# Activations placed 96 bytes (modulo 256) from the weights in SBUF, in place of 192

## The chip, the cores and the metric

The kernel is one program on one core of a Trainium2 chip. The metric is the device time of one execution in microseconds. The two timed runs of the kernel before took 2176.17 and 2174.1 us, median 2175.14 us.

## The reference, cut to what matters

A batch of one, 256 tokens, model width 2048, everything in float32, passes through three layers in a row:

```python
def reference(x, ...):
    x = first_block(x, ...)         # mLSTM + gated conv mixer, w_out, conv FFN (D_FF 5504), norm
    x = second_block(x, ...)        # GLA mixer, then MLA attention, each x + rms_norm(y)
    return x

# the bulk of it is products of 256 tokens with float32 weights, such as
proj = hn @ w_in + b_in                       # 2048 -> q, k, v, o, gates, conv parts, merge gates
h = h + merged @ w_out
u = causal_dwconv(hn @ w_up, ffn_conv_w, ffn_conv_b)
h = h + (silu(gate) * val) @ w_down
proj = h @ l0_gla_w_in;  y = (o * silu(gate)) @ l0_gla_w_out
proj = h @ l1_mla_w_in;  y = (o * silu(gate)) @ l1_mla_w_out
```

The weights are about 390 MB of float32 and each is used once.

## The kernel before, in words

**Layout.** Features lie on the 128 partitions and the 256 tokens (`T`) along the free dimension. An activation of 2048 features is `[P, 16, 256]` float32; feature tile k is 1024 contiguous bytes in each partition.

**Weights.** The host lays all weights out as one stream of 370 chunks of 1 MB (`stream_in`), in the order of use. SyncE loads chunk after chunk into `raw` (L533). A chunk is two units of `[128, 1024]` float32, a unit is eight weight tiles of 128x128. ScalarE rounds each unit to `w_hi` in the format fp32r (L955), and VectorE writes the rest, `raw - w_hi`, to `w_lo` (L1385). `raw`, `w_hi` and `w_lo` are rings of four units. The activations are split in the same manner into a high and a low part (`n_hi`/`n_lo`, `mg_hi`/`mg_lo`, `f_hi`/`f_lo`, `og_hi`/`og_lo`, `c_hi`/`c_lo`, `mo_hi`/`mo_lo`, `hm_*`, `yc_*`).

**The products.** The function `tile` (L574 to L576) makes one weight tile's product of three matmuls into the same PSUM bank: high weights by high activations, high weights by low activations, low weights by high activations. Each matmul loads its own 128x128 stationary operand (a weight tile; 512 bytes in each partition) and streams 256 columns of activations (1024 bytes in each partition). This is called a triple below. `feature_tile` strings 16 such triples together, and its helpers the others. `token_tiles` (L619 to L621) does the values of the mixers the other way round: the activation tile is stationary and 256 or 512 columns of weights stream. The small attention products (`att`) are plain float32 matmuls.

**The order.** It is written out by hand on each engine, in the order of the table `PHASES`: gates, mix (four heads), merge, wout, wup, wdown, rank, gla (four heads), glaout, latent, krope, mla (four groups), mlaout. TensorE waits for the split of a weight unit (`lo_ready`), for activations, and for its PSUM bank to be emptied (`acc_taken`).

**Addresses.** The tensors made with `sb` (L111 to L132) follow one another in each partition: `x`, `raw`, `w_hi`, `w_lo`, then the filler `apart`, which nothing reads or writes, then `n_hi`, `n_lo`, the parameters and the small constants. Each of the large ones is a multiple of 256 bytes long. `x` starts at byte 16512, which is 128 modulo 256, and so do `raw`, `w_hi` and `w_lo`. `apart` is 192 bytes, so `n_hi` and `n_lo` start at 64 modulo 256. All other tensors are placed by `Arena` from `arena_start` (L135) on, which is rounded up to 64 modulo 256 (byte 130368); their sizes are nearly all multiples of 256 bytes, so every activation that streams also starts at 64 modulo 256. `LINE` is 256. `par` is 2296 bytes and is followed at 64 modulo 256 again by `normed`, `square` and the rest; `ones`, `ident` and `ones_r` lie 64 bytes further (after `g_both`).

Of the kernel before, what the change touches and what calls it, by code (L numbers as in the profile page):

```python
# [18 lines left out]
P = 128  # L19
# [18 lines left out]
LINE = 256  # L38
# [29 lines left out]
def program(nc, x_in, stream_in, params_in, v_bias_in, gk2_in, positions_in, out):  # L68
# [26 lines left out]
    with ctx:  # L95
        def sb(name, shape, dt=fp32):
            return ctx.enter_context(nc.sbuf_tensor(name, shape, dt))
# [14 lines left out]
        raw = sb("raw", [P, RING, UNIT])  # L112
        w_hi = sb("w_hi", [P, RING, UNIT], fp32r)
        w_lo = sb("w_lo", [P, RING, UNIT], fp32r)
        apart = sb("apart", [P, LINE // 4 * 3 // 4])
        n_hi = sb("n_hi", [P, KT, T], fp32r)
        n_lo = sb("n_lo", [P, KT, T], fp32r)
        par = sb("par", [P, N_PARAMS])
# [13 lines left out]
        eps_eps_col = sb("eps_eps_col", [P, 1])  # L132


        arena_start = -(-(nc.sbuf_base - LINE // 4) // LINE) * LINE + LINE // 4  # L135
        arena_end = nc.sbuf_usable_end

        class Arena:
# [2163 lines left out]
```

How the kernel before makes its waits and increments, by code:

```python
        def taken(eng, b, name, i, j):  # L465
            eng.wait_ge(acc_taken[b], FREE + count(1 + b, name, i, j + 1))
# [32 lines left out]
            def wait(self):  # L501
                self.eng.wait_ge(self.steps, self.n if self.i is None else self.i * self.per + self.n)
# [19 lines left out]
        @block.sync  # L522
# [7 lines left out]
            def load(n, slot, source):  # L530
                sp.wait_ge(lo_ready, 2 * n - 2)
                sp.dma_start(raw[:, 2 * slot:2 * slot + 2, :],
                             stream_in[source].rearrange("p (u n) -> p u n", u=2)).then_inc(raw_ready[slot], 16)
# [5 lines left out]
                    load(2 * i + c, c, 2 * i + c)  # L540
            with sp.Fori(0, A_HEADS // 4) as i:
                for c, source in enumerate((2, 0, 1, 3, 4, 5, 6, 7)):
                    load(8 * i + (mla_at + c), c % 2, 8 * i + (mla_at + source))
            with sp.Fori(mla_end // 2, N_CHUNKS // 2) as i:
                for c in range(2):
                    load(2 * i + c, c, 2 * i + c)
            for g in range(KT // 4):
                sp.wait_ge(x_added, FREE + KT // 4 + g + 1)
                sp.wait_ge(x_added_pool, FREE + KT // 4 + g + 1)
                sp.dma_start(out[:, 4 * g:4 * g + 4, :], x[:, 4 * g:4 * g + 4, :]).then_inc(stored, 16)
            sp.wait_ge(stored, 16 * (KT // 4))
# [4 lines left out]
            def unit(name, i, j):  # L558
                u, s, _ = unit_of(name, i, j)
                pe.wait_ge(lo_ready, u + 1)
                return s
# [307 lines left out]
            def scores(i, n):  # L870
                pe.wait_ge(qrope_ready, FREE + 8 * i + 4 * (n // 2 + 1))
```

## Time and profile before

| | |
|---|---|
| median of the timed runs | 2175.14 us |
| the profiled execution | 2177.88 us, its span 2175.8 us |
| mean granted TensorE clock | 0.987 |
| busy, share of the span: TensorE / weight loads / VectorE / ScalarE / GpSimd | 97% / 95% / 60% / 53% / 13% |
| DMA | 393.83 MB, mean 181 GB/s, queue busy 50.4% |
| triples by their activations (matmuls at L574) | `n` 3488, `f` 688, `og`, `mo` and `mg` 256 each, `c` 160, `hm` and `yc` 128 each: 5360 in all |
| matmuls of `token_tiles` | 384 of 256 columns, 480 of 512 columns |

Two things help in reading it. A matmul's record lasts from its start to the end of its passage through the array, while the next one starts long before: what a matmul costs in a dense stream is the step from one start to the next, and that is the length of a stretch divided by the matmuls that started in it. The lines of the trace count in a stretch also the two or three matmuls that were under way when it began. And the granted clock has two levels, 1.00 (2.4 GHz) and 0.50 (1.2 GHz).

### The profile page before, as it was taken

To read this page: it belongs to the slowest core of one execution; us is meant where nothing else is said; L and a number is where in the kernel's file an instruction comes from. 1 tells how busy PE (TensorE), PEld (TensorE's weight loads), DVE (VectorE), ACT (ScalarE), POOL (GpSimd) and SP (SyncE) were. 2 spreads that over 40 slices of the span, in tenths; PEclk is the share of its full clock that TensorE was granted. 3 is DMA by queue.
4 is the path that set the end of the run, shared out by engine and by line. 5 is a ranking of instruction groups with operands and counts; after the bars stand their busy time and mean duration, and the time that the engine had idled before them with its cause. 6 is when DMAs were issued, how large, how long until landed. Compare 5 with 4: busy or idle time off the path is not lost.

```text
span 2175.8 us, 46737 instructions
## 1 busy us (share of the span) xinstructions
PE 2110.0 (97%) x17596; PEld 2071.1 (95%) x17596; DVE 1313.0 (60%) x1662; ACT 1159.3 (53%) x1558; POOL 280.0 (13%) x325
## 2 busy tenths in 40 slices
PE   5999999999999999999999999999999979999996
PEld 5999999999999999999999999999998969999996
DVE  5656655444457777777775555575665565766644
ACT  5444545555445656565655444645555445566643
POOL 2000000000110111111111101111001123111112
PEclk8999999999999999999999999999999989999998
DMA  4455455555555555555555655455444533444443
GB/s 153 170 179 190 172 175 197 185 200 193 185 188 206 193 193 193 193 193 193 193 193 195 224 218 209 173 180 194 174 158 171 192 135 136 175 154 156 171 174 116
DMA packets 54927, 393.83 MB, mean 181 GB/s; under 512 B 6097, under 2 KB 6225, under 8 KB 7522
## 3 DMA queue, kind: packets, MB, share of 16 engines
q1 hardware_dynamic: 54432, 392.19, 50.4%
q10 hardware_dynamic: 450, 1.02, 0.1%
q8 instruction: 31, 0.51, 0.1%
q14 instruction: 14, 0.11, 0.0%
HBM read 391.09 MB, written 2.10 MB: 181 GB/s over the span
## 4 chain that ended last, share of the span: by engine, by line
PE 83%; issue 11%; DVE 2%; POOL 2%; ACT 1%; DMA 0%; DVEq 0%; POOLq 0%; ACTq 0%; SPq 0%
PE acc L574 24%; PE acc L575 24%; PE acc L576 24%; PE tok L619 2%; PE tok L621 2%; PE tok L620 2%; POOL sumsq_g L1983 1%; PE att L647 1%; POOL n_lo L1992 0%; PE att L878 0%; PE att L879 0%; POOL x L2005 0%; DVE w_lo L1385 0%; DVE rstd L1393 0%; PE att L821 0%
## 5 line engine op out<-in xcount | busy, mean ns | idle before, releaser
L1385 DVE TENSOR_TENSOR w_lo<-raw,w_hi 128x1024 fp32r<-128x1024 f32 x740 | 904.1, 1235 | 710.9 <-ACT w_hi L955 708.5
L955 ACT ACTIVATE w_hi<-raw 128x1024 fp32r<-128x1024 f32 x740 | 768.3, 1056 | 552.1 <-PE acc L576 295.1
L574 PE MATMUL acc<-n_hi,w_hi 128*128 128x256 f32 x3488 | 974.2, 279 | 23.9 <-POOL n_lo L1992 20.3
L575 PE MATMUL acc<-n_lo,w_hi 128*128 128x256 f32 x3488 | 968.7, 278 | 0.0
L576 PE MATMUL acc<-n_hi,w_lo 128*128 128x256 f32 x3488 | 968.6, 278 | 0.0
L574 PEld LDWEIGHTS acc<-n_hi,w_hi 128*128 128x128 f32 x3488 | 658.9, 189 | 27.3 <-issue 20.5
L575 PEld LDWEIGHTS acc<-n_lo,w_hi 128*128 128x128 f32 x3488 | 659.7, 189 | 0.5
L576 PEld LDWEIGHTS acc<-n_hi,w_lo 128*128 128x128 f32 x3488 | 658.9, 189 | 0.0
L574 PE MATMUL acc<-f_hi,w_hi 128*128 128x256 f32 x688 | 189.9, 276 | 0.0
L575 PE MATMUL acc<-f_lo,w_hi 128*128 128x256 f32 x688 | 189.9, 276 | 0.0
L576 PE MATMUL acc<-f_hi,w_lo 128*128 128x256 f32 x688 | 189.9, 276 | 0.0
L576 PEld LDWEIGHTS acc<-f_hi,w_lo 128*128 128x128 f32 x688 | 129.2, 188 | 0.0
L574 PEld LDWEIGHTS acc<-f_hi,w_hi 128*128 128x128 f32 x688 | 129.2, 188 | 0.0
L575 PEld LDWEIGHTS acc<-f_lo,w_hi 128*128 128x128 f32 x688 | 129.2, 188 | 0.0
L2059 POOL TENSOR_TENSOR f_lo<-f_act,f_hi 128x256 f32 x43 | 57.8, 1344 | 413.7 <-ACT f_hi L1142 413.7
L1981 POOL TENSOR_TENSOR sumsq<-sumsq,square 128x256 f32<-128x256 f32 x64 | 47.3, 739 | 436.5 <-ACT square L964 228.7
L619 PE MATMUL tok<-w_hi,n_hi 128*128 128x256 f32 (+1 forms) x256 | 86.8, 339 | 0.0
L621 PE MATMUL tok<-w_hi,n_lo 128*128 128x256 f32 (+1 forms) x256 | 86.7, 339 | 0.0
L620 PE MATMUL tok<-w_lo,n_hi 128*128 128x256 f32 (+1 forms) x256 | 86.6, 338 | 0.0
L574 PE MATMUL acc<-og_hi,w_hi 128*128 128x256 f32 x256 | 72.0, 281 | 2.4 <-DVE og_lo L1696 2.4
L574 PE MATMUL acc<-mo_hi,w_hi 128*128 128x256 f32 x256 | 72.0, 281 | 0.0
L575 PE MATMUL acc<-mo_lo,w_hi 128*128 128x256 f32 x256 | 71.9, 281 | 0.0
(324 smaller groups left out, 2959.7 us busy)
## 6 DMA issues: line engine op xcount, KB each, us to landing
raw<-stream_in SPq DMA_DIRECT2D x370, 1024.0 KB, 4.8
x<-x_in SPq DMA_DIRECT2D x4, 512.0 KB, 7.6
out<-x SPq DMA_DIRECT2D x4, 512.0 KB, 2.7
v_bias<-v_bias_in ACTq DMA_DIRECT2D x1, 512.0 KB, 8.9
par<-params_in ACTq DMA_DIRECT2D x1, 287.0 KB, 5.5
pos_i<-positions_in ACTq DMA_DIRECT2D x1, 128.0 KB, 6.8
gk<-gk_in ACTq DMA_DIRECT2D x1, 68.0 KB
```

What stands on the lines that cost most here:

```text
L574: nc.tensor.matmul(out, w_hi[:, s, wc], hi[:, k, :], start=first, stop=False)
L575: nc.tensor.matmul(out, w_hi[:, s, wc], lo[:, k, :], start=False, stop=False)
L576: return nc.tensor.matmul(out, w_lo[:, s, wc], hi[:, k, :], start=False, stop=last)
L619: nc.tensor.matmul(o, hi[:, k0 + k, tt], w_hi[:, s, wc], start=k == 0, stop=False)
L620: nc.tensor.matmul(o, hi[:, k0 + k, tt], w_lo[:, s, wc], start=False, stop=False)
L621: last = nc.tensor.matmul(o, lo[:, k0 + k, tt], w_hi[:, s, wc], start=False, stop=k == n_k - 1)
L647: last = nc.tensor.matmul(att[3][:, 0:T], ones[:, :], squares_all[:, k, :], start=k == 0, stop=k == KT - 1)
L955: nc.scalar.activation(w_hi[:, s, :], raw[:, s, :], ACT.Copy).then_inc(hi_ready, 1)
L1385: nc.vector.tensor_tensor(w_lo[:, s, :], raw[:, s, :], w_hi[:, s, :].bitcast(fp32), ALU.subtract).then_inc(lo_ready, 1)
L1981: ins = gp.tensor_tensor(sumsq[:, :], sumsq[:, :], square[:, m, :], ALU.add)
L1983: ins = gp.tensor_tensor(sumsq_g[:, :], sumsq_g[:, :], square_g[:, m, :], ALU.add)
L2059: gp.tensor_tensor(f_lo[:, i, :], f_act[:, :], f_hi[:, i, :].bitcast(fp32), ALU.subtract)\
```

## The change

The filler becomes 96 bytes, and the arena's start is rounded up to 224 modulo 256 in place of 64:

```diff
         w_lo = sb("w_lo", [P, RING, UNIT], fp32r)
-        apart = sb("apart", [P, LINE // 4 * 3 // 4])
+        apart = sb("apart", [P, LINE // 4 * 3 // 8])
         n_hi = sb("n_hi", [P, KT, T], fp32r)
...
-        arena_start = -(-(nc.sbuf_base - LINE // 4) // LINE) * LINE + LINE // 4
+        arena_start = -(-(nc.sbuf_base - LINE * 7 // 8) // LINE) * LINE + LINE * 7 // 8
```

`x`, `raw`, `w_hi` and `w_lo` stay where they are (128 modulo 256). `n_hi`, `n_lo` and all that follows them, and the whole arena, move down by 96 bytes: the arena starts at byte 130272 in place of 130368, and the streamed activations at 224 modulo 256 in place of 64. Relative to the weights that is 96 in place of 192. Where the weights stream and the activation is stationary (`token_tiles`), the distance from stationary to streamed operand goes from 64 to 160. Distances between two tensors of the arena, and between `n_hi` and `ones`, stay as they were. No instruction is added, removed or moved on any engine, and each queue issues the same transfers in the same order.

## Rows read from the trace of the kernel before

**Rows 1.** The page: the span; busy time, share and instructions of the engines.
```profile
span 2175.8 us, 46737 instructions
PE 2110.0 (97%) x17596; PEld 2071.1 (95%) x17596; DVE 1313.0 (60%) x1662; ACT 1159.3 (53%) x1558; POOL 280.0 (13%) x325
```

**Rows 2.** The page: the chain that ended last, by engine.
```profile
PE 83%; issue 11%; DVE 2%; POOL 2%; ACT 1%; DMA 0%; DVEq 0%; POOLq 0%; ACTq 0%; SPq 0%
```

**Rows 3.** Groups of instructions: xcount, busy us, mean ns of one, idle before.
```profile
L574 PE MATMUL acc<-n_hi,w_hi 128*128 128x256 f32 x3488 | 974.2, 279 | 23.9 <-POOL n_lo L1992 20.3 <-issue 3.6
L575 PE MATMUL acc<-f_lo,w_hi 128*128 128x256 f32 x688 | 189.9, 276 | 0.0
L575 PE MATMUL acc<-og_lo,w_hi 128*128 128x256 f32 x256 | 71.9, 281 | 0.0
```

**Rows 4.** By stretch: us, then PE, PEld, DVE, ACT, POOL busy (x); clock, DMA.
```profile
44.00:308.00 264.00, 263.43 (x2199) 258.76 (x2199) 156.98 (x183) 130.91 (x164) 15.50 (x13) 0.99 0.49 174
310.00:1382.00 1072.00, 1072.00 (x9461) 1072.00 (x9460) 658.70 (x814) 586.34 (x748) 120.00 (x130) 1.00 0.55 197
1403.00:1681.00 278.00, 277.81 (x2100) 259.43 (x2098) 174.14 (x240) 147.94 (x182) 29.53 (x20) 1.00 0.50 178
1684.00:1768.00 84.00, 84.00 (x716) 84.00 (x715) 41.50 (x45) 39.66 (x60) 11.11 (x15) 1.00 0.53 188
1803.00:2065.00 262.00, 258.14 (x2038) 250.41 (x2039) 166.29 (x246) 156.55 (x259) 50.79 (x80) 1.00 0.45 162
2067.00:2156.00 89.00, 89.00 (x758) 89.00 (x758) 34.29 (x29) 38.92 (x60) 12.50 (x18) 1.00 0.43 153
```

**Rows 5.** Timeline of TensorE from 799.7 us (start us, length us), wup stage.
```profile
799.74 0.28 PE L575 MATMUL acc<-n_lo,w_hi 128*128 128x256 f32 x1
799.85 0.28 PE L576 MATMUL acc<-n_hi,w_lo 128*128 128x256 f32 x1
...
800.53 0.28 PE L576 MATMUL acc<-n_hi,w_lo 128*128 128x256 f32 x1
```

**Rows 6.** Timeline of the weight loads in the same stretch.
```profile
799.85 0.19 PEld L574 LDWEIGHTS acc<-n_hi,w_hi 128*128 128x128 f32 x1
...
800.53 0.19 PEld L574 LDWEIGHTS acc<-n_hi,w_hi 128*128 128x128 f32 x1
```

**Rows 7.** Timeline of TensorE from 40.1 us, granted clock 0.50.
```profile
40.11 0.41 PE L576 MATMUL acc<-n_hi,w_lo 128*128 128x256 f32 x1
...
41.39 0.41 PE L576 MATMUL acc<-n_hi,w_lo 128*128 128x256 f32 x1
```

**Rows 8.** Groups at L575 in the stretches 44:308, 1403:1681 and 1803:2065.
```profile
L575 PE MATMUL acc<-n_lo,w_hi 128*128 128x256 f32 x573 | 159.3, 278 | 0.0
...
L575 PE MATMUL acc<-n_lo,w_hi 128*128 128x256 f32 x488 | 134.9, 276 | 0.0
...
L575 PE MATMUL acc<-n_lo,w_hi 128*128 128x256 f32 x408 | 113.6, 278 | 0.0
L575 PE MATMUL acc<-c_lo,w_hi 128*128 128x256 f32 x160 | 44.8, 280 | 0.0
```

**Rows 9.** Timeline of TensorE from 307.8 us: the last small product before the long stretch.
```profile
307.30 0.60 PE L695 MATMUL att<-h_sum,ones 128*128 128x256 f32 x2
...
308.08 0.28 PE L574 MATMUL acc<-n_hi,w_hi 128*128 128x256 f32 x1
308.21 0.28 PE L575 MATMUL acc<-n_lo,w_hi 128*128 128x256 f32 x1
308.32 0.28 PE L576 MATMUL acc<-n_hi,w_lo 128*128 128x256 f32 x1
```

**Rows 10.** Timeline of TensorE from 1419.8 us: `token_tiles` of 512 columns.
```profile
1419.76 0.39 PE L619 MATMUL tok<-w_hi,n_hi 128*128 128x512 f32 x1
...
1420.91 0.39 PE L621 MATMUL tok<-w_hi,n_lo 128*128 128x512 f32 x1
```

**Rows 11.** VectorE's groups that read from one and two elements off a tile's start.
```profile
L1619 DVE SCALAR_TENSOR_TENSOR f_val<-f_pre,par,f_val 128x255 f32<-128x255 f32 x43 | 20.6, 478 | 0.0
L1623 DVE SCALAR_TENSOR_TENSOR f_val<-f_pre,par,f_val 128x254 f32<-128x254 f32 x43 | 20.8, 483 | 6.1 <-DVE f_val L1619 0.2
```

## The prediction

> **What bounds the kernel now.** I read the page first. TensorE is busy 97% of the span with 17596 matmuls [rows 1], and the chain that ended last runs 83% through it, with 11% of issue, which here is time between matmuls that waited for nothing [rows 2]. TensorE's idle time before the largest group is 23.9 us of the whole [rows 3]. So the time is the number of matmuls times the step from one start to the next, and the change can act only through that step, or through a wait that does not exist now.
>
> Next come the stretches [rows 4]. From 310 to 1382 us (merge, wout, wup, wdown) TensorE never stops: 1072 us for 9461 matmuls less the three already under way, a **fast step of 113.3 ns**. From 1684 to 1768 us (glaout) it never stops either, and there it is 84 us for 713: a **slow step of 117.8 ns**. From 2067 to 2156 us (mlaout), 89 us for 755, it is 117.9 ns. The granted clock is 1.00 in all three. The timeline shows the fast step at close hand, seven steps in 0.79 us [rows 5], with a weight load starting beside every matmul [rows 6]. The record of one matmul lasts 276 ns at the fast step and 281 ns at the slow one, as the groups of `f` and `og` show [rows 3], and that tells the two apart where a stretch is mixed.
>
> What is the least such a step could be? At a granted clock of 0.50 the same matmuls start every 213.3 ns (1.28 us for six [rows 7]), which is exactly 256 columns at 1.2 GHz. At 2.4 GHz the columns alone would be **106.7 ns**. So 6.7 ns of the fast step and 11.1 ns of the slow one are something that doesn't show at half the clock. `f`, `mg` and `og` all start at the same address modulo 256 and are used by the same code, yet two steps exist, and each is kept for hundreds or thousands of matmuls. The step is thus not set by addresses alone: the stream falls into one of two rhythms, and changes it at an interruption. The long fast stretch began right after a small product, with one odd step of 0.13 us [rows 9], and the rhythm then held until 1382 us.
>
> **How many matmuls run at which step.** 5360 triples are 16,080 matmuls. Fast are the 9,458 of the long stretch and the gla stretch's 488 x 3 = 1,464, whose records last 276 ns. In the mix stretch the mean is 159.3 / 573 = 278.0 ns, so (281 - 278.0) / 5 = 60% of 1,719 are fast, 1,031; in the mla stretch 113.6 / 408 = 278.4 gives 52% of 1,224, 636, and `c` at 280 gives 20% of 480, 96 [rows 8]. That is 12,685 fast. About 110 ran at half the clock at the beginning and between stages. The other 3,285 are slow.
>
> **The change, part by part.**
> - *Instructions, queues, waits:* nothing is added, removed or moved, so there is no term.
> - *VectorE, ScalarE, GpSimd operands, 96 bytes lower:* VectorE's operations that begin one and two elements off a tile's start last 478 and 483 ns [rows 11], so an odd start shows no price. And they are covered: those engines are busy 60, 53 and 13% [rows 1]. Were each a few per cent longer, TensorE would still not wait in the dense stretches. I take nothing.
> - *The weight stream:* `raw`, `w_hi`, `w_lo` stay. Its transfers fill 0.55 of the DMA engines' time in the dense stretch [rows 4], so a quicker TensorE would be fed too.
> - *The matmul's two reads:* stationary and streamed operand are read at once, and their distance modulo 256 goes from 192 to 96, for `token_tiles` from 64 to 160. This is the only term, and the trace holds no matmul of this kind at the new distance. I bound it from both sides. Below: nothing but the columns, 106.7 ns. That saves 12,685 x 6.7 + 3,285 x 11.1 = 121 us; the 480 products of 512 columns, which now take 1.15 us for five, 230 ns each [rows 10], against 213.3 for their columns, save 8 us more, and those of 256 columns some 4: 133 us. Above: the largest step in a running stream in my rows, the odd one of 0.13 us at 308.08 (0.125 to 0.13 by the rounding, and I take 123 ns, the middle of it and the slow step). All of them at that would cost 12,685 x 9.7 + 3,285 x 5.2 = 140 us. The value I take is the nearest row, which is the same matmul at the old distance: the two steps stay as they are. It is nearest since 64 and 192, the two distances that now exist, appear to give steps of the same kind, each with a few per cent above the columns.
>
> By that the sum is 2177.9 us for the profiled execution, plus or minus the reshuffling of rhythms in the interrupted stages; on the scale of the median, which is 2.7 us lower, 2175.
>
> **Rule against row.** The rows show a step 6.7 or 11.1 ns above the columns at full clock and none at half clock [rows 4, 7]. The Trainium skill ("SBUF — State Buffer", Who interferes with whom, and "TensorE: Matmul & The Clock Gate", Part 2) says that TensorE has two independent read ports, one for the moving operand and one for the weight load, and that it never waits on anyone. By that rule the change is worth nothing and the time stays. The same TensorE page gives 256 / 2.4 + 2.5 = 109.2 ns for a warm matmul of 256 columns, an estimate by which the sum would be 4 to 9 ns per matmul too high now; the trace does not show that step in any dense stretch, and two different steps at one address speak against the rule that nothing interferes.
>
> **The rivals.**
> - *The placement does nothing (N).* The excess comes from how matmul and load hand over, and addresses have no part. For it: `og` and `f` lie at the same place modulo 256 and have different steps. Against it: nothing in the trace varies the distance alone, so it can't be excluded. Time 2174 to 2177 us.
> - *The long stretch falls into the slow rhythm (S), the other side.* The place is the first uninterrupted feature tile after the product at 307.30 us, in the last mixer head. The new distance shifts when the two reads meet, and if the stream after it settles at 117.8 ns, 9,458 matmuls pay 4.45 ns: 42 us, 2217 on the median's scale. If the gla stretch and the rest settle there as well, 12,685 x 4.45 = 56 us, 2231. It decides from some 9,800 matmuls changed to slow on (43.5 us, 2%). For it: glaout and mlaout are slow from their first matmul to the last. Against: four interruptions of the same kind in the mixer ended fast.
> - *A step above both (U).* 96 is no multiple of 64, while 192 and 64 are, and the streamed tile then begins in the middle of a 64-byte piece counted from the weights. If the reads meet once more per matmul, at the price at which fast and slow differ, all pay 4.45 ns: 15,970 x 4.45 = 71 us and 4 for `token_tiles`, 2250; by the upper bound 2315. No row speaks for it but the odd step.
> - *A step below both (D).* The reads meet once less: 75 us less, 2100; by the lower bound 2042. For it: two rhythms 4.45 ns apart look like rungs, and the fast one is still 6.7 ns above the columns, so a rung of 108.9 has room. Against it: 9,458 matmuls in a row never found it at the old distance.
> - *The same two steps (F, the forecast).* All fast would be 3,285 x 4.45 = 15 us less, 2161; some more slow ones than now in the mixer and MLA stages, 2190.
>
> **How the numbers follow.** F 0.27, N 0.16, S 0.24 (0.07 for the long stretch alone, which is 1.9%, and 0.17 for more), U 0.13, D 0.20 (of it 0.02 for a mild form within 2%). What a measurement can tell from no change is about 2%, here 43.5 us: below 2131.6 or above 2218.6. Faster: 0.18. Within: 0.27 + 0.16 + 0.07 + 0.02 = 0.52. Slower: 0.17 + 0.13 = 0.30. F and N lead to the same time, which is the predicted one, **2175 us**. The range must take in S and the nearer half of D: 2090 to 2250. It leaves out the strong form of D, 0.06, and most of U, 0.10. F and N alone would be 2155 to 2195.
>
> **What would show it.** In the profile of the changed kernel the number of matmuls that start in the stretch from merge to wdown, divided into its length, is the whole test: 113.3 ns is F or N, 117.8 is S, about 122 is U, about 109 is D. The records there would last 276, 281, more or less than these. If F holds, glaout and mlaout may have changed their step. For N all stages keep their own step, mix and MLA to within a few matmuls. In every case the idle time before the main groups, the granted clock and the stages' busy counts on VectorE and ScalarE should stay; should TensorE wait for `w_lo` or `w_hi` in the dense stretch, or VectorE's and ScalarE's durations have moved by more than 1%, the step that costed them at nothing is wrong. At half the clock the step should stay 213.3 ns. The prediction is wrong if the dense stretch runs at a step that is not one of the two.

## The result and the profile after

The changed kernel takes 2269.43 us (two runs, 2269.19 to 2269.68) against 2175.14 us: a ratio of 1.0423, 95% interval 1.04 to 1.0446. It is slower by 94.3 us, outside the range of 2090 to 2250, and the forecast of no change was wrong.

The page of the changed kernel, the lines to hold against [rows 1, 3]:

```profile
span 2267.6 us, 46737 instructions
PE 2203.7 (97%) x17596; PEld 2163.7 (95%) x17596; DVE 1315.8 (58%) x1662; ACT 1160.7 (51%) x1558; POOL 278.6 (12%) x325
...
L574 PE MATMUL acc<-n_hi,w_hi 128*128 128x256 f32 x3488 | 993.8, 285 | 22.2 <-POOL n_lo L1992 18.0
```

TensorE has 93.7 us more busy time with the same instructions; the other engines' busy time moved by less than 3 us, and the idle time before the largest group is 22.2 us where it was 23.9. So nothing waits that did not wait before: the matmuls themselves come slower. By stretch (us, then PE, PEld, DVE, ACT, POOL busy with counts; clock, DMA), to be held against [rows 4]:

```profile
310.00:1440.00 1130.00, 1130.00 (x9418) 1129.95 (x9417) 660.45 (x812) 586.20 (x746) 118.69 (x128) 1.00 0.52 186
...
2160.00:2235.00 75.00, 75.00 (x627) 75.00 (x627) 30.45 (x26) 34.34 (x52) 9.64 (x13) 1.00 0.51 182
```

Merge to wdown: 1130 us / 9415 starts = **120.0 ns**, where it was 113.3. Inside mlaout 75 us / 624 starts gives 120.2, and the starts themselves average 120.0, where the step was 117.9. The clock is 1.00 as before. The two rhythms are gone: everywhere in the program the 256-column triples run at a mean of 120.0 while the clock is full. It is a pattern that repeats every six matmuls, in the long stretch with steps of 125, 116, 123, 119, 121 and 116 ns. The timeline of TensorE (start, length) shows such a group of six:

```profile
45.04 0.28 PE L574 MATMUL acc<-n_hi,w_hi 128*128 128x256 f32 x1
...
45.52 0.28 PE L575 MATMUL acc<-n_lo,w_hi 128*128 128x256 f32 x1
45.63 0.29 PE L576 MATMUL acc<-n_hi,w_lo 128*128 128x256 f32 x1
45.76 0.28 PE L574 MATMUL acc<-n_hi,w_hi 128*128 128x256 f32 x1
```

Six steps in 0.72 us, of 0.11 to 0.13. At half the clock nothing changed. The same kernel at a granted clock of 0.50, six steps in 1.28 us, 213.3 ns each, as in [rows 7]:

```profile
40.01 0.41 PE L576 MATMUL acc<-n_hi,w_lo 128*128 128x256 f32 x1
...
41.29 0.41 PE L576 MATMUL acc<-n_hi,w_lo 128*128 128x256 f32 x1
```

**The sum.** Counting starts in the trace before, about 12,657 matmuls ran at the fast step and 3,256 at the slow one. To 120.0 they pay 12,657 x 6.67 = 84.4 and 3,256 x 2.2 = 7.2 us; the 480 products of 512 columns went from 231.4 to 236.5 ns on average (up to the next start, whatever it is), 2.4 us. Together that is 94.0 us. The medians differ by 94.3, the spans of the two traces that the counts come from by 91.8 (2267.6 less 2175.8), so the sum is right to some 2 us, not to tenths.

### The profile page after: what moved, and what is told of

Read it like the earlier page. It is cut to its first block, busy times and chain, and to the rows that moved or that the text cites. A ratio compares the mean times of both kernels' runs of the same rounds, so it can differ in the third digit from the quotient of the medians.

```text
span 2267.6 us, 46737 instructions
## 1 busy us (share of the span) xinstructions
PE 2203.7 (97%) x17596; PEld 2163.7 (95%) x17596; DVE 1315.8 (58%) x1662; ACT 1160.7 (51%) x1558; POOL 278.6 (12%) x325
## 4 chain that ended last, share of the span: by engine, by line
PE 84%; issue 11%; DVE 2%; POOL 2%; ACT 1%; DMA 1%; DVEq 0%; POOLq 0%; ACTq 0%; SPq 0%
PE acc L576 24%; PE acc L574 24%; PE acc L575 24%; PE tok L619 2%; PE tok L620 2%; PE tok L621 2%; POOL sumsq_g L1983 1%; POOL n_lo L1992 0%; PE att L647 0%; PE att L878 0%; PE att L879 0%; POOL x L2005 0%; DVE rstd L1393 0%; PE att L821 0%; PE att L896 0%
## 5 line engine op out<-in xcount | busy, mean ns | idle before, releaser
L1385 DVE TENSOR_TENSOR w_lo<-raw,w_hi 128x1024 fp32r<-128x1024 f32 x740 | 904.5, 1234 | 754.5 <-ACT w_hi L955 752.5
L955 ACT ACTIVATE w_hi<-raw 128x1024 fp32r<-128x1024 f32 x740 | 768.7, 1055 | 589.2 <-PE acc L576 365.5
L574 PE MATMUL acc<-n_hi,w_hi 128*128 128x256 f32 x3488 | 993.8, 285 | 22.2 <-POOL n_lo L1992 18.0
L576 PE MATMUL acc<-n_hi,w_lo 128*128 128x256 f32 x3488 | 990.6, 284 | 0.0
L575 PE MATMUL acc<-n_lo,w_hi 128*128 128x256 f32 x3488 | 983.6, 282 | 0.0
L575 PEld LDWEIGHTS acc<-n_lo,w_hi 128*128 128x128 f32 x3488 | 666.2, 191 | 0.5
L576 PEld LDWEIGHTS acc<-n_hi,w_lo 128*128 128x128 f32 x3488 | 657.6, 189 | 0.0
L576 PE MATMUL acc<-f_hi,w_lo 128*128 128x256 f32 x688 | 194.7, 283 | 0.0
L575 PE MATMUL acc<-f_lo,w_hi 128*128 128x256 f32 x688 | 192.8, 280 | 0.0
L575 PEld LDWEIGHTS acc<-f_lo,w_hi 128*128 128x128 f32 x688 | 130.8, 190 | 0.0
L576 PEld LDWEIGHTS acc<-f_hi,w_lo 128*128 128x128 f32 x688 | 128.7, 187 | 0.0
L576 PE MATMUL acc<-mg_hi,w_lo 128*128 128x256 f32 x256 | 72.4, 283 | 0.0
L576 PE MATMUL acc<-mo_hi,w_lo 128*128 128x256 f32 x256 | 72.4, 283 | 0.0
```

The source lines that it names most:

```text
L574: nc.tensor.matmul(out, w_hi[:, s, wc], hi[:, k, :], start=first, stop=False)
L575: nc.tensor.matmul(out, w_hi[:, s, wc], lo[:, k, :], start=False, stop=False)
L576: return nc.tensor.matmul(out, w_lo[:, s, wc], hi[:, k, :], start=False, stop=last)
L955: nc.scalar.activation(w_hi[:, s, :], raw[:, s, :], ACT.Copy).then_inc(hi_ready, 1)
L1385: nc.vector.tensor_tensor(w_lo[:, s, :], raw[:, s, :], w_hi[:, s, :].bitcast(fp32), ALU.subtract).then_inc(lo_ready, 1)
```

## The experiments

Two theories are put to the test. **T1, distance**: the step goes by the distance modulo 256 between the stream and the load that runs beside it. **T2, alignment**: a streamed tile that starts at 32 modulo 64 costs more, wherever the weights are.

**d192_all32 and d96_all32: everything moved up by 32 bytes.** This leaves the distances and swaps which kernel has its streams at 32 modulo 64.

```diff
+        lead = sb("lead", [P, 32 // 4])
         raw = sb("raw", [P, RING, UNIT])
...
-        apart = sb("apart", [P, LINE // 4 * 3 // 4])
+        apart = sb("apart", [P, 192 // 4])     # d96_all32: 96 // 4; the arena at 96, or at 0
```

> Distance 192 kept, but weights and activations both moved up by 32 bytes, so that the streamed activations start at 32 modulo 64. Theory T1 (only the distance between the two operands modulo 256 counts): steps of 113.3 and 117.8 ns, 2165 to 2190 us. Theory T2 (a streamed tile that starts at 32 modulo 64 is what costs, whatever the distance): 120.0 ns everywhere in the dense stretch, about 2269 us.

> Distance 96 kept, everything moved up by 32 bytes, so that the activations start at 0 modulo 256 and the weights at 160. T1: 120.0 ns, about 2269 us. T2: back to 113.3 and 117.8 ns, about 2175 us.

Measured 2175.21 us (ratio 1.0009, interval 0.9997 to 1.002) and 2269.53 us (1.0433, 1.0403 to 1.0464). The stretch from 700 to 1100 us, inside wup, of the first and then of the second; 400 us divided by the count less three:

```profile
700.00:1100.00 400.00, 400.00 (x3531) 400.00 (x3531) 288.36 (x407) 238.28 (x313) 50.18 (x37) 1.00 0.55 193
```
```profile
700.00:1100.00 400.00, 400.00 (x3336) 400.00 (x3335) 273.89 (x383) 225.91 (x297) 46.19 (x35) 1.00 0.52 183
```

113.4 and 120.0 ns. T2 falls, since alignment was swapped and each kernel kept the time of its distance.

**The sweep: d0, d32, d64, d128, d160, d224, and d448.** Each sets the filler to that many bytes and the arena to the same place modulo 256. Steps finer than 32 bytes were not tried.

```diff
-        apart = sb("apart", [P, LINE // 4 * 3 // 4])
+        apart = sb("apart", [P, 64 // 4])       # d64; d0 has none
...
-        arena_start = -(-(nc.sbuf_base - LINE // 4) // LINE) * LINE + LINE // 4
+        arena_start = -(-(nc.sbuf_base - 192) // LINE) * LINE + 192
```

> Distance 64, weights where they were, activations at 192 modulo 256. T2: 113.3 and 117.8 ns, about 2175 us, like every distance that is a multiple of 64. T1 does not say which step, only that it is this distance's own; before, the 256-column products with weights streaming had distance 64 and ran at 117.8 ns, so 117.8 everywhere, about 2230 us, is its guess.

> Distance 160, activations at 32 modulo 256. T2: 120.0 ns, about 2269 us. T1: a step of its own; if the step is the same for a distance and for its mirror image (160 is 256 less 96), 120.0 and 2269 us as well. A step near 109 ns would give 2100 us.

> Distance 0, the filler left out. So far the step in the stretch from merge to wdown is 117.8 ns at 64, 120.0 at 96, 117.3 at 160, 113.3 at 192. A smooth curve over the distance (theory: the place in the matmul at which the two reads meet sets the price) would put 0 between 113 and 118: 115, about 2195 us. Theory that operands beginning in the same place collide at every start: above 120, over 2270 us.

> Distance 32. Smooth curve: some 116 ns, 2210 us. Same-start theory: best when far from 0, so 32 is worse than 64: above 117.8, over 2235 us.

> Distance 128, between the two measured neighbours 96 (120.0 ns) and 160 (117.3 ns). Smooth curve: near the top of it, 119 ns, about 2260 us. Same-start theory: the farthest from 0 and so the best, 113 ns or less, 2175 us or less.

> Distance 224. Smooth curve: the low point is somewhere from 192 to 256, so 113.3 ns or a step below it, down to 109: 2100 to 2175 us. Same-start theory: worse than 192, 118 ns or more, over 2230 us.

> A filler of 448 bytes: distance 192 plus 256. If the price has a period of 256 bytes: 113.3 ns from merge to wdown, 2165 to 2190 us. If the true distance in bytes counts, or a longer period: another step, between 115 and 120 ns, 2195 to 2270 us.

| distance | median us | ratio to before, interval | matmuls counted, 700 to 1100 us | step there |
|---|---|---|---|---|
| 0 | 2266.94 | 1.0411 (1.0389 to 1.0432) | 3336 | 120.0 |
| 32 | 2218.35 | 1.0187 (1.0166 to 1.0209) | 3431 | 116.7 |
| 64 | 2232.85 | 1.0265 (1.0235 to 1.0295) | 3399 | 117.8 |
| 96 (the change) | 2269.43 | 1.0423 (1.04 to 1.0446) | 3335 | 120.0 |
| 128 | 2249.38 | 1.033 (1.0309 to 1.0351) | 3374 | 118.7 |
| 160 | 2234.08 | 1.027 (1.0241 to 1.03) | 3411 | 117.4 |
| 192 (before) | 2175.14 | | 3532 | 113.3 |
| 224 | 2243.71 | 1.0302 (1.0285 to 1.0319) | 3383 | 118.3 |
| 448 = 192 + 256 | 2178.17 | 1.0004 (0.999 to 1.0018) | 3532 | 113.3 |

Each ratio is to runs of the kernel before that were timed beside that version, with medians of 2174.49 to 2176.80 us. At 32 the change is clear of zero, but whether it reaches 2% is not.

The last row of the table shows that 448 behaves as 192 does, as a period of 256 bytes would have it. Between 0 and 256 the curve is not smooth: 192 stands alone, with 117.4 and 118.3 on its two sides, and neither my smooth curve nor the guess that the farthest from 0 is best held. The mirror image did not hold either (96 against 160). Only 192 has the rhythm of 113.3 for most of the program.

Nor is 192 the only distance with more than one step. In d160 the starts give 117.3 ns from merge to wdown, 118.7 in glaout and mlaout, and 120.0 in one stretch of the mla stage.

**The same law with the parts swapped.** Nothing was forecast for this; it is read from the traces of the sweep. `token_tiles` is in them too, and there the weights stream while the activation is loaded, so its distance is 256 less that of the triples. In each mixer head but the first, its 256-column products run 96 in a row. Their step by their starts, beside that of the triples at the same distance:

| distance | 0 | 32 | 64 | 96 | 128 | 160 | 192 | 224 |
|---|---|---|---|---|---|---|---|---|
| triples | 120.0 | 116.7 | 117.8 | 120.0 | 118.7 | 117.4 | 113.3 and 117.8 | 118.3 |
| `token_tiles` | 120.0 | 116.7 | 117.8 | 119.9 | 118.7 | 117.3 | 113.5 and 117.8 | 118.3 |
| from | d0 | d224 | before | d160 | d128 | after | d64 | d32 |

Here the streamed weights never move, so where the stream itself begins is not what counts; the signed distance is, with either kind of data on either side. Even the two rhythms come back at 192. In d64 they take turns from head to head. A piece of the second head in d160 (120.0 ns), and of the second and the third in d64, 9 us with 75, 76 and 79 starts:

```profile
133.00:142.00 9.00, 9.00 (x78) 9.00 (x77) 2.82 (x4) 4.24 (x7) 0.00 (x0) 1.00 0.40 131
...
132.00:141.00 9.00, 9.00 (x79) 9.00 (x78) 2.96 (x4) 4.24 (x7) 0.00 (x0) 1.00 0.39 131
204.00:213.00 9.00, 9.00 (x82) 9.00 (x81) 3.26 (x4) 4.25 (x7) 0.00 (x0) 1.00 0.39 126
```

**n96: the filler alone**, the arena left at distance 192.

> One part of the change alone: the filler is 96 bytes, so the normed activations are 96 from the weights, while the arena stays at 192. Theory T1 (each matmul's step goes by the distance of its own two streams): 120.0 ns for the 10,464 matmuls that stream the normed activations, 113.3 or 117.8 for the 5,616 that stream the others: 2175 + 10,464 x 5.7 = about 2235 us. Rival (something in the whole layout): all or nothing, 2175 or 2269 us.

Measured 2237.24 us (ratio 1.0287, 1.0258 to 1.0317). In one and the same kernel, the stretch of wup, which streams `n`, and one inside wdown, which streams `f`:

```profile
700.00:1100.00 400.00, 400.00 (x3335) 400.00 (x3335) 274.71 (x384) 226.43 (x297) 46.00 (x34) 1.00 0.51 183
1220.00:1320.00 100.00, 100.00 (x885) 100.00 (x884) 52.43 (x55) 49.88 (x63) 10.06 (x14) 1.00 0.58 216
```

120.0 ns and 100 / 882 = 113.4 ns. Each matmul pays for its own operands. The filler alone is 62 of the 94 us; that leaves 32 for the arena, which was not run alone.

**wlo96: distance 96 for `w_lo` alone.**

```diff
+        gap = sb("gap", [P, 96 // 4])
         w_lo = sb("w_lo", [P, RING, UNIT], fp32r)
-        apart = sb("apart", [P, LINE // 4 * 3 // 4])
+        apart = sb("apart", [P, 96 // 4])
```

> 32 * 3 bytes of filler put before w_lo, and the same taken from the filler after it: activations are 192 from w_hi as before and 96 from w_lo. Of a triple one load in three reads w_lo: it runs beside the second matmul's stream if a load overlaps the matmul before its own, and beside the third's if it overlaps its own. Next-load theory: the second matmul's start-to-start step (low activations) grows towards 120 and the others stay near 113.3. Own-load theory: the third's grows. Either way the triple is some 347 ns and the time about 2175 + 5,360 x 6 = 2205 us. Theory that a load takes no part: 113.3 and 2175 us.

One run, 2236.99 us. The groups from 720 to 1100 us (xcount, busy us, mean ns; the inserted line moved the numbers by one, so L576 is the second matmul of the triple):

```profile
L576 PE MATMUL acc<-n_lo,w_hi 128*128 128x256 f32 x1077 | 306.9, 285 | 0.0
L577 PE MATMUL acc<-n_hi,w_lo 128*128 128x256 f32 x1076 | 300.2, 279 | 0.0
L575 PE MATMUL acc<-n_hi,w_hi 128*128 128x256 f32 x1076 | 298.1, 277 | 0.0
```

By their starts, the second matmul's step is 123.3 ns, the others' 114.2 and 115.8. The second streams low activations, 192 from its own weights in `w_hi`; what lies 96 away is `w_lo`, which is loaded for the third. So in this run the load that counts is the **next** matmul's, which fits the records of the trace, where that load starts beside the matmul before its own [rows 5, 6]. It is one run, and wlo_d160 below does not bear the rule out. The size was off: the triple takes 353.3 ns, where I expected 347.

**wfix96, wfix0, sfix96, bfix0, bfix96: a read held at one place.** The edit of one of the three lines of `tile`, with both changes in one picture; the other two lines are changed alike.

```diff
-                nc.tensor.matmul(out, w_hi[:, s, wc], hi[:, k, :], start=first, stop=False)
+                nc.tensor.matmul(out, w_hi[:, s, c * P:c * P + 1].to_broadcast([P, P]),    # wfix, bfix
+                                 hi[:, k, 0:1].to_broadcast([P, T]), ...)                  # sfix, bfix
```

> At distance 96, every weight load of the triples reads the tile's first column 128 times (a stride of zero) in place of walking through 512 bytes; the product is not the reference's. Theory T1 (the walk of the load and the walk of the stream meet): the number of meetings changes, so the step leaves 120.0; with the load at one place it falls to 113 or less, 2175 us or less. Rival (the step is set by the stream alone, by where it begins): still 120.0, 2269 us.

> At distance 96, the streamed operand of the triples is one column read 256 times (a stride of zero), and the load walks as before; the product is not the reference's. T1: the step leaves 120.0 and falls to 113 or less. Rival (the load alone sets it): still 120.0. Rival (a fixed hand-over cost per matmul and nothing else): 120.0 too.

> Distance 0 (120.0 ns with both walking), with the load held at one place as it was in the run at distance 96 that gave 113.33 ns; the product is not the reference's. If the distance counts only while both walk: 113.33 ns again, about 2177 us. If it counts for a held load too: another step.

> Distance 0, both reads of a triple's matmuls held at one place (stride zero for the load and for the stream), and those two places have the same address modulo 256; the product is not the reference's. Theory T1 as a clash of addresses modulo 256: the two reads clash all the time and the step is far above 120 ns. Theory that only a walk makes a load or stream costly (each new piece has to be fetched): lowest step of all, 111.7 ns or less, about 2145 us or less, the same as at distance 96.

> The same at distance 96: the two places never have the same address modulo 256. T1 as a clash: they never meet, 107 to 112 ns, 2070 to 2145 us. Walk theory: the same step as at distance 0.

One run each: wfix96 2177.05, wfix0 2175.02, sfix96 2145.27, bfix0 2140.39, bfix96 2144.79 us. The stretch from 700 to 1100 us of wfix96, of sfix96, and of bfix0:

```profile
700.00:1100.00 400.00, 400.00 (x3532) 400.00 (x3531) 288.63 (x407) 238.68 (x315) 50.13 (x37) 1.00 0.54 193
```
```profile
700.00:1100.00 400.00, 400.00 (x3584) 400.00 (x3584) 290.61 (x411) 241.80 (x318) 50.76 (x38) 1.00 0.55 196
```
```profile
700.00:1100.00 400.00, 400.00 (x3585) 400.00 (x3584) 290.45 (x412) 241.87 (x319) 50.32 (x38) 1.00 0.54 196
```

In this stretch the load held gives 113.3 ns at distance 96 and at distance 0 alike (x3532 in both), where both walking gives 120.0. With the stream held, or both, it is 111.7 ns. bfix0 and bfix96 have the same count (x3585), although in bfix0 both reads stay at the same address modulo 256 all the time; their times differ by 4 us, one run each. So my picture of a clash whenever the two are at equal addresses was wrong: that alone costs nothing. And the 120.0 ns of this stretch need both reads to walk: hold the load, and 6.7 ns go at 0 and at 96; hold the stream, at 96, and 8.3 ns go.

The long stretch is not the whole program, though. By the starts in wfix96, one stretch of 143 triple steps in each mixer head averages 120.0 ns although the load is held, and the gla stage 116.7. A piece of each:

```profile
78.00:92.00 14.00, 14.00 (x119) 14.00 (x118) 8.43 (x9) 6.54 (x8) 1.26 (x1) 1.00 0.46 160
...
1465.00:1485.00 20.00, 20.00 (x174) 20.00 (x173) 14.39 (x22) 11.74 (x16) 1.98 (x1) 1.00 0.46 162
```

In wfix0 the head's stretch is at 120.0 too, as is one in the mla stage, and the gla stage is mostly at 113.3. So a walking stream has several rhythms (113.3, 116.7 and 120.0) even beside a held load; the distance is not the only thing that can make a step of 120.0, and holding the load does not take every trace of it away. With the stream held (sfix96, bfix0, bfix96) there is one step, 111.7 ns, in every stretch of full clock. So several rhythms are seen only where the stream walks. At 192 the walking load reaches the 113.3 of the held one in the long stretch; no read was held at distance 192 itself.

**wlo_d160 and wlo_d224: another distance for `w_lo` alone**, as in wlo96.

> w_lo moved by 32 bytes, the activations kept 192 from w_hi, so that only the second matmul of a triple (which streams while w_lo is loaded) has distance 160. If the step goes by the pair that overlaps, as in the run at 96: the second matmul's step is near the 117.3 ns of distance 160 or somewhat above, the others 113 to 116: a triple of 344 ns or more, 2190 to 2215 us. Rival: the mixture breaks the slow rhythm of 117.8 ns and the interrupted stages gain up to 15 us: 2161 us at the least, with 113.3 in the long stretch.

> The same with distance 224 for the second matmul alone. By the pair: its step near the 118.3 ns of distance 224, a triple of 345 ns or more, 2190 to 2220 us. Rival as for 160: 2161 us.

Measured 2246.1 us (1.032, 1.0302 to 1.0337) and 2254.02 us (1.0354, 1.0337 to 1.0372), worse than distance 160 or 224 for all three matmuls. From 700 to 1100 us:

```profile
700.00:1100.00 400.00, 400.00 (x3367) 400.00 (x3366) 276.82 (x387) 230.22 (x301) 46.08 (x34) 1.00 0.51 184
```
```profile
700.00:1100.00 400.00, 400.00 (x3336) 400.00 (x3336) 275.03 (x383) 226.71 (x297) 45.70 (x34) 1.00 0.51 183
```

118.9 and 120.0 ns. All three steps of a triple grew, not the second's alone: first to third 117.9, 118.3 and 120.4 ns in wlo_d160, and 119.4, 120.5 and 120.1 in wlo_d224. So here the rule "each pair has its price" fails, and with it the neat reading of wlo96: in wlo_d160 the largest step is that of the matmul that uses `w_lo`, not of the one before it. That the distance to the load counts is shown; which of the three steps pays when the distances are mixed is not. No version that keeps the product is faster than the kernel before.

## Why the prediction was wrong

- **What bounds the kernel** was right. The time is the number of matmuls times their step, and the other engines' stretches did not matter.
- **No term for instructions, for the other engines' operands, for the weight stream:** right, and shown by the durations. ScalarE's split takes 1055 ns where it took 1056, VectorE's 1234 for 1235.
- **The failed step** is the one on the two reads: "The value I take is the nearest row, which is the same matmul at the old distance". It costed a change of distance by a row in which the distance had not changed. The runs showed in its place a price that goes by the distance, 120.0 ns at 96 where it is 113.3 or 117.8 at 192. The measured term is +94 us, inside the bracket of -133 to +140 that I had worked out, and I gave it as 0.
- The reason I gave for it, that 64 and 192 "appear to give steps of the same kind", is not borne out. With 64 for the triples the long stretch runs at 117.8 ns and with 192 at 113.3. The trace before had the hint: distance 64 was there in the 256-column products with streaming weights, and in every mixer head they ran at the slow 117.8 while most triples ran fast.
- **Rival U, a step above both**, came nearest: it had 2250 at one step of 4.45 ns and 2315 at the upper bound. It got 0.13, and most of it lay outside the range. Its reason, that 96 is no multiple of 64, was wrong: the distances 0 and 128 are multiples and cost 120.0 and 118.7 ns, while 32 and 160 are none and cost 116.7 and 117.4. Its signs did not fit its sum either. A price of 4.45 ns on a fast step of 113.3 makes 117.8, the step that I had listed as the sign of S; the 122 listed for U is the slow step with that price.
- **Rival S** named the right sign and the wrong mechanism: the stream did not fall into the old slow rhythm, it has a new one. Even its full form, 2231, was 38 us short.
- **Rival N** is refuted. The Trainium skill ("SBUF — State Buffer", Who interferes with whom) says that TensorE's two read ports are independent and that TensorE waits on no one; by that rule all eight distances would give one step, and they give 113.3 to 120.0 ns. The measurement decides. The other page cited, "TensorE: Matmul & The Clock Gate", gives an estimate of 109.2 ns for 256 columns. No run here shows it; the lowest step is 111.7, with the stream held.
- **Rival D** had no rung to stand on. The room below 113.3 was taken from the columns alone (106.7 ns), and no stretch of any run with a walking stream went below 113.3, with the load walking or held. The lower bound of the bracket was a step that the kernel reached at none of the eight places.

What stays open: why the stream has several rhythms at one placement (at 192, at 160, and beside a held load), what makes it choose one, and what makes 192 the one good place of eight. In the long stretch the steps repeat every six matmuls at 96 and every five at 160, and at 0 each is 120; this, and that mixing distances spoils all three steps, suggests that a matmul's start depends on those before it, but no run isolates how.

## What to carry to other kernels

Where every matmul of a dense stream loads its own weights, the address of the streamed operand relative to the weights was worth up to 6% of the step here and is free to set: place it, sweep all eight places of 32 bytes within 256, and read the step (stretch divided by starts) instead of trusting a curve between two points. When a change moves a quantity that the profile shows at one value only, the row at the old value is no price for the new one; the likeliest case must come from the bracket, and a bracket of both signs is a reason to keep both ends in the range.

## What the runs showed of the hardware

- 256-column fp32r matmuls with a load each, at the full granted clock: a step of 113.3 ns at best and 120.0 at worst, by the distance modulo 256 from the loaded to the streamed operand, and the same whether activations stream or weights do. At half the clock the step is 213.3 ns at all eight distances.
- The absolute place did not matter (all shifted by 32 bytes: 2175.21 us at distance 192, 2269.53 at 96), and 256 more bytes of distance did not either (1.0004).
- A load held at one place brings the long stretch to 113.3 ns at distances 0 and 96, but stretches of 116.7 and 120.0 remain elsewhere. A stream held at one place gives 111.7 ns in all stretches of triples (load walking: distance 96; load held: 0 and 96).
- For 512 columns the order is another: 229.6 ns on average at distance 0 (d0), 231.4 in the kernel before (distance 64), 236.5 in the changed one (160). The best filler for one kind of product is not the best for the other.
